# Branch blocks of a decoder layer: three joined products per block in banks of their own, summed over halves before the gates

## The reference, cut to what matters

```
merged = (jax.nn.sigmoid(ga) * (ya @ w_br_a[l])
          + jax.nn.sigmoid(gb) * (yb @ w_br_b[l])
          + jax.nn.sigmoid(gc) * (yc @ w_br_c[l]))
x = x + merged @ w_out[l]
```

## Time and profile before

| what | us |
|---|---|
| median of 3 runs | 2014.06 (2010.58 to 2015.64) |
| the profiled execution, its own time | 2014.7 |
| its span, first to last instruction | 2013.4 |
| TensorE busy in the span | 1774.1 (88%) |
| VectorE busy | 1555.3 (77%) |
| ScalarE busy | 932.5 (46%) |
| GpSimd busy | 650.5 (32%) |
| the branch blocks, start of the first and of the last matmul | 547.5 and 641.0 |

### The profile page before, as it was taken

One profiled execution on the slowest core, in us unless ns is written; L12 is line 12 of the kernel. 1 busy time (PEld: TensorE's weight loads), 2 busy tenths in 40 slices (PEclk: granted clock), 3 DMA queues, 4 the chain that ended last, 5 costly groups with the idle time before them and its releaser, 6 DMA issues.

```text
span 2013.4 us, 26324 instructions
## 1 busy us (share of the span) xinstructions
PE 1774.1 (88%) x9788; PEld 1532.3 (76%) x9788; DVE 1555.3 (77%) x2067; ACT 932.5 (46%) x1482; POOL 650.5 (32%) x558
## 2 busy tenths in 40 slices
PE   6999999999999999956776244499999999999998
PEld 5878888888899887756776244488888888888886
DVE  5575555555565548988988899988988989999997
ACT  5444444444543442123443899843444444343344
POOL 1000000001045003467777677122222224353452
PEclk9999999999999999978888555799999999999999
DMA  9556565656566869999999999588999999999995
GB/s 313 171 161 170 171 177 170 172 171 177 146 187 210 321 228 417 366 406 403 417 397 410 375 388 403 217 332 353 411 411 388 396 398 404 406 406 408 401 410 204
DMA packets 293970, 627.79 MB, mean 312 GB/s; under 512 B 10412, under 2 KB 223453, under 8 KB 235390
## 3 DMA queue, kind: packets, MB, share of 16 engines
q0 software_dynamic: 48400, 343.95, 42.3%
q1 hardware_dynamic: 244846, 281.15, 40.6%
q10 hardware_dynamic: 640, 1.63, 0.2%
HBM read 622.45 MB, written 8.44 MB: 313 GB/s over the span
## 4 chain that ended last, share of the span: by engine, by line
PE 68%; DVE 12%; ACT 5%; issue 5%; POOL 4%; DVEq 3%; DMA 3%; ACTq 0%; POOLq 0%
PE ps L2124 34%; PE ps L1767 12%; PE ps L1766 6%; DVE u_ring L1559 6%; PE ps L1966 4%; PE ps L1952 4%; DVEq L1509 3%; DMA u_ring<-in_peer_u,idx_all 2%; PE ps L1754 1%; PE ps L1763 1%; ACT ones L1157 1%; ACT w_hi L798 1%; POOL u_ring L718 1%; POOL u_ring L709 1%; PE ps L1891 1%
## 5 line engine op out<-in xcount | busy, mean ns | idle before, releaser
L1767 PE MATMUL ps<-act_both,w_hi 128*128 128x512 f32 x1200 | 427.1, 398 | 0.0
L1214 ACT ACTIVATE v_hi<-v_raw 128x2048 fp32r<-128x2048 f32 x128 | 245.6, 1919 | 388.8 <-PE ps L2124 198.2
L2124 PE MATMUL ps<-v_hi,c_hi 128*128 128x512 f32 x1008 | 392.2, 389 | 1.2 <-DVE c_lo L1638 1.2
L2124 PE MATMUL ps<-v_lo,c_hi 128*128 128x512 f32 x1008 | 392.1, 389 | 0.0
L2124 PE MATMUL ps<-v_hi,c_lo 128*128 128x512 f32 x1008 | 392.1, 389 | 0.0
L1300 DVE TENSOR_TENSOR w_lo<-raw,w_hi 128x2048 fp32r<-128x2048 f32 x111 | 257.2, 2317 | 159.9 <-ACT w_hi L798 159.8
L1559 DVE CUSTOM_DVE_ANT_0 u_ring<-u_ring,ps 128x2048 f32<-128x2048 f32 x144 | 326.2, 2277 | 21.9 <-DMA u_ring<-in_peer_u,idx_all 21.7
L798 ACT ACTIVATE w_hi<-raw 128x2048 fp32r<-128x2048 f32 x112 | 214.3, 1913 | 269.0 <-PE ps L1767 205.8
L1766 PE MATMUL ps<-act_both,w_lo 128*128 128x256 f32 x1200 | 338.4, 282 | 0.0
L1634 DVE TENSOR_TENSOR v_lo<-v_raw,v_hi 128x2048 fp32r<-128x2048 f32 x128 | 293.2, 2290 | 53.3 <-ACT v_hi L1214 52.7
L1767 PEld LDWEIGHTS ps<-act_both,w_hi 128*128 128x128 f32 x1200 | 226.7, 189 | 50.2
(11 more groups left out here) (265 smaller groups left out, 2693.6 us busy)
## 6 DMA issues: line engine op xcount, KB each, us to landing
v_raw<-in_peer_v SPq DMA_DIRECT2D x128, 1024.0 KB, 7.2
raw<-in_w_in SPq DMA_DIRECT2D x80, 1024.0 KB
raw<-in_w_out SPq DMA_DIRECT2D x16, 1024.0 KB
wq<-in_peer_w_q SPq DMA_DIRECT2D x8, 2048.0 KB, 11.3
raw<-in_w_br_a SPq DMA_DIRECT2D x16, 512.0 KB
bias_by_query<-bias_by_distance POOLq DMA_DIRECT2D x1, 4096.0 KB, 20.7
bias_st<-bias_by_query POOLq DMA_DIRECT2D x16, 256.0 KB, 4.7
raw<-in_w_br_b SPq DMA_DIRECT2D x16, 256.0 KB
```

The source lines that it names most:

```text
L1214: nc.scalar.activation(v_hi[hi_slot(b)][:, :], v_raw[b % RING][:, :], ACT.Copy).then_inc(vh_ok, 1)
L1767: last = nc.tensor.matmul(bank, *both, start=False, stop=(k == NK - 1))
L2124: last = nc.tensor.matmul(ps[:, 4 * t + c, :], c_parts[cp][j % v_slots[0]][:, t], v_parts[vp][j % v_slots[vp]][:, WIDE * c:WIDE * c + WIDE ...
```

## The change

- TensorE takes `by_pairs` for the branch blocks too: for each `k` one matmul of 512 columns and one of 256. Each branch has a bank of its own, banks 0 to 2 for even blocks and 3 to 5 for odd ones.
- VectorE reads the three banks with one `tensor_reduce`, which adds the halves and writes 768 elements a partition into `mtmp`. A new semaphore, `mj_ok`, tells TensorE after it that the banks are free (before: `m_mul`, after the products). A `drain` follows, and then one instruction multiplies gates and sums, both in SBUF, in place (`m_mul`).
- The low part of merged block `m` moves behind the low weights of the next block (`merged_low`); the last one stands behind the loop.
- GpSimd's and ScalarE's instructions and waits, SP's transfers, and TensorE's wait for all of `m_mul` behind block 15, are as before.

```diff
+        def merged_low(m, j):
+            dve.wait_ge(m_hi, m + 1)
+            nc.vector.scalar_tensor_tensor(out=mg_lo[:, span(T * m, T)], in0=msum[:, j], scalar=0.5,
+                                           in1=mg_hi[:, span(T * m, T)].bitcast(F32), op0=ALU.mult, op1=ALU.subtract).then_inc(m_lo, 1)
         def merge(i):
             for j in range(NRAW):
                 m = NRAW * i + j
                 dve.wait_ge(blk_done, m + (N_BR + 1))
                 wait(dve, m_sum, 2 * m - 2)
-                nc.vector.scalar_tensor_tensor(out=mtmp[:, j % 2, 0:2].rearrange("p g t -> p (g t)"), in0=gates[:, span(3 * T * m, 2 * T)],
-                                               scalar=1.0, in1=ps[:, J + j % 2, :], op0=ALU.add, op1=ALU.mult)
-                nc.vector.scalar_tensor_tensor(out=mtmp[:, j % 2, 2], in0=gates[:, span(3 * T * m + 2 * T, T)], scalar=1.0,
-                                               in1=ps[:, S_BANK + j % 2, 0:T], op0=ALU.add, op1=ALU.mult).then_inc(m_mul, 1)
+                nc.vector.tensor_reduce(mtmp[:, j % 2], ps[:, 3 * (j % 2):3 * (j % 2) + 3].rearrange("p g (h t) -> p g t h", h=2), AX.X,
+                                        ALU.add).then_inc(mj_ok, 1)
+                dve.drain()
+                products = mtmp[:, j % 2].rearrange("p g t -> p (g t)")
+                nc.vector.scalar_tensor_tensor(out=products, in0=gates[:, span(3 * T * m, 3 * T)], scalar=1.0, in1=products,
+                                               op0=ALU.add, op1=ALU.mult).then_inc(m_mul, 1)
                 low(NRAW * i + N_BR, j + 2)
-                dve.wait_ge(m_hi, m + 1)
-                nc.vector.scalar_tensor_tensor(out=mg_lo[:, span(T * m, T)], in0=msum[:, j], scalar=0.5,
-                                               in1=mg_hi[:, span(T * m, T)].bitcast(F32), op0=ALU.mult, op1=ALU.subtract).then_inc(m_lo, 1)
+                if not isinstance(m, int) or m > 0:
+                    merged_low(m - 1, (j - 1) % NRAW)
         peeled(dve, NK // NRAW, merge)
+        merged_low(NK - 1, NRAW - 1)
...
-                wait(pe, m_mul, NRAW * i + (j - 1))
+                wait(pe, mj_ok, NRAW * i + (j - 1))
...
-                by_column(ps[:, J + j % 2, 0:T], j % NHL, 0, 8, waits)
-                by_column(ps[:, J + j % 2, T:2 * T], j % NHL, 8, 12, waits)
-                by_column(ps[:, S_BANK + j % 2, 0:T], j % NHL, 12, NK, waits).then_inc(blk_done, 1)
+                by_pairs(ps[:, 3 * (j % 2)], j % NHL, 0, 8, waits)
+                by_pairs(ps[:, 3 * (j % 2) + 1], j % NHL, 8, 12, waits)
+                by_pairs(ps[:, 3 * (j % 2) + 2], j % NHL, 12, NK, waits).then_inc(blk_done, 1)
```

More of the change, by code:

```diff
@@ L411, in build @@
     y_lo = sem("y_lo")
+    mj_ok = sem("mj_ok")
     m_mul = sem("m_mul")
@@ L1746, in _, with wide_part @@
         w_wide = [w[:, :, :, :].rearrange("p s (a b) c -> p s a (b c)", b=WIDE // P) for w in w_parts]
[L1748 to L1758, removed]
+        def wide_part(bank, slot, k, k0=0, k1=NK):
             both, low_part = (w_hi[:, slot, k], act_both[:, k]), (w_lo[:, slot, k], act_hi[:, k])
-            if k == 0:
+            if k == k0:
                 nc.tensor.matmul(bank, *both, start=True, stop=False)
@@ L1766, in wide_part, with by_pairs @@
                 nc.tensor.matmul(bank[:, 0:T], *low_part, start=False, stop=False)
-                last = nc.tensor.matmul(bank, *both, start=False, stop=(k == NK - 1))
+                last = nc.tensor.matmul(bank, *both, start=False, stop=(k == k1 - 1))
             return last
-        def by_pairs(bank, slot):
-            for k in range(NK):
-                last = wide_part(bank, slot, k)
+        def by_pairs(bank, slot, k0=0, k1=NK, waits=None):
+            for k in range(k0, k1):
+                if waits is not None:
+                    waits(k)
+                last = wide_part(bank, slot, k, k0, k1)
             return last
```

## The result

| | before | after |
|---|---|---|
| median, us | 2013.39 (4 runs, 2010.58 to 2015.64) | 2027.11 (4 runs, 2026.52 to 2027.57) |
| the profiled execution's own time, us | 2014.7 | 2026.52 |
| its span, us | 2013.4 | 2025.2 |
| start of the projection, us | 642.57 | 649.44 |

The ratio is 1.0069, with a 95% interval of 1.0056 to 1.0082: the change makes the kernel some 14 us slower, where 6.8 were predicted. The time lies 0.1 us beyond the upper end of the range.

A forecast was written before the change was run, and what follows sets the result against it. TensorE was taken to bound the stage, busy 93.25 of 94.0 us. Blocks +3.1, end +2.2 and clock +1.5 made +6.8 on 2014.7: 2021.5, lowered 0.6 for the runs' median to 2020.9 us; range 2013 to 2027.

The forecast's parts named there:

- Matmuls, 5.60 us a block: TensorE's branch blocks: 5.60 us each with 512- and 256-column pairs, 0.16 less, 2.6 us over 16 blocks if TensorE keeps pace.
- Drain 0.07: VectorE, between reduction and products: the drain costs 0.07 us, an estimate between 0 and 0.1.
- Merged low part 0.35: VectorE, right behind low weights: 0.42 us less 0.07 overlap, assuming instructions issued back to back keep the port.
- Rival 2: GpSimd gets in between low weights and merged low part: 0.45 every second block, 2.7 us, giving 2023.6; chance 0.20.
- Two rings, 6.0 us a block: Branch blocks: from late high weights, ScalarE's ring of 5.86 and VectorE's of 6.03 exceed TensorE's 5.60; thirteen blocks add 3.2 us.
- The loop's starts, +0.9, less 0.5 for the first stalls: VectorE's 0.29 us at each of three loop starts joins its ring, +0.9; first stalls still growing take 0.5 off.
- The end, +2.2: TensorE's wait for block 15's products before the projection grows from 1.32 to 3.5 to 3.8 us: +2.2.
- The clock, +1.5 (0 to 3): Projection start: after 3.5 us idle TensorE runs at half clock for about 3 us, costing 1.5, bounds 0 and 3.
- The projection behind absorbs nothing: The projection behind the stage is paced by TensorE, so nothing in it absorbs the delay.
- TensorE keeps pace (0.22): Branch blocks: TensorE still sets the pace, as sums find gaps or VectorE's part is shorter; 2013.3 to 2014.8, chance 0.22.
- Weight loads (0.05): TensorE's blocks: weight loads are the limit, not columns; if a block falls to 5.2 us, 2007; chance 0.05.
- A clock that falls inside the stage (0.03): Half clock on a tenth of the stage's 94 us costs 5 us more: 2027; chance 0.03.

The follow-up runs named there:

- low_first: end_and_act with VectorE's next low weights between reduction and products, and a wait for `mj_ok` in place of the drain; 2015.94 us, ratio 1.0023.
- act_order: Kernel after, with ScalarE's high part of merged block m - 1 moved behind the high weights of block m + 2; 2019.79 us, ratio 1.0030.
- short_sums: Kernel after, with both GpSimd sums covering 16 of their 256 columns and `msum` cleared once ahead; 2016.13 us, ratio 1.0013.
- end_filler: Kernel after, with 14 unneeded matmuls between TensorE's last block and its wait for the products; 2020.77 us, ratio 1.0042.
- end_wait: Kernel after, with TensorE's wait before the projection on block 14's sum over halves instead of all products; 2023.07 us, ratio 1.0048.
- defer_only: Kernel before, with only the merged low part moved a block later; 2011.58 us against 2011.37 for before, ratio 1.0005.
- end_and_act: Kernel after with the edits of end_wait and act_order together; 2014.81 us, ratio 1.0027.
- end_wout: end_wait with the first `w_out` piece of the projection's second column group issued ahead of `x`, `g_ffn` and sub keys; 2017.18 us, ratio 1.0035.
- low_first_wout: low_first with the load order of end_wout; 2010.63 us against 2012.09 for before, ratio 0.9996.

## Why the prediction was wrong

**Step by step.**

- *Matmuls, 5.60 us a block:* right. *low_first* shows TensorE without idle and blocks 5.62 apart (592.42 less 586.80).
- *Reduction 1.76, products 0.96:* right (1745 and 959 ns).
- *Drain 0.07:* right in the pass with fixed numbers (1.83 us from the start of the reduction to that of the products, 565.60 to 567.43), too small by 0.1 in the loop. There, from the start of the reduction to that of the products it is 1.93 us, with 0.18 marked as issue. In *low_first*, which has no drain, the instruction behind the reduction starts after 1.84 (626.10 to 627.94). That is 0.1 us a block in VectorE's ring.
- *Merged low part 0.35 (0.42 less overlap):* this is **the step that failed**. It rested on the assumption that "instructions issued back to back keep the port". It is written in both rings and in VectorE's own 5.3. Measured: 0.95 in 15 of 16 blocks, because GpSimd's waiting sum gets the port between two VectorE instructions that follow each other at once. VectorE's ring without any wait is then 5.88 and not 5.3, shown by *act_order* (5.88 in every block), *short_sums* (0.44, stage 96.6) and *low_first* (0.42, stage 92.6). Rival 2 named this mechanism with a chance of 0.20, and priced it for every second block, at 0.45: 2.7 us in all. It is 0.53 in every block but the last, and that its 2.7 comes near the 2.9 that were missing is luck (next point).
- *Two rings, 6.0 us a block:* ScalarE's high weights do stand behind `mg_hi`, behind GpSimd's sum, but they hold VectorE up in every second block and not in each. The ring of 6.03 holds for those blocks: with 0.5 more for the merged low part and 0.1 for the drain it gives the 6.65 measured. In the others the high weights are there in time, the 0.67 for GpSimd's gap drops out, and VectorE's ring runs at 5.89. So the port and the drain cost some 0.6 us a block more than forecast, the alternation gave back 0.77 in every second one, and the mean of 6.27 is only 0.26 above the forecast 6.01 because two errors of opposite sign met. Over 13 blocks that is 3.4 us.
- *The loop's starts, +0.9, less 0.5 for the first stalls:* not borne out. At the three starts the reduction comes 0.87 us behind the start of the merged low part (602.15 to 603.02, for one), as in every other block: they cost nothing. The blocks cost +6.0 us (8.3 less 2.3) instead of +3.1; the 2.9 between them is, to 0.1, the 3.4 less the 0.4 of this term.
- *The end, +2.2:* right. The idle time is 3.64 instead of 1.32, +2.3.
- *The clock, +1.5 (0 to 3):* the mechanism was right, the term mis-sized: 2.4 us by *end_filler*. I had taken the 3 us of half clock at 547.5 for the length; here it was 5.6.
- *The projection behind absorbs nothing:* right for the delay itself. For a gain it is different: the projection of *end_wait* starts earlier and takes 5.4 us more than that of before (2.8 more than after, which itself has 2.4 of slow clock), and mostly the loads decide it.

The sum so corrected is 6.0 + 2.3 + 2.4 = 10.7, against 10.9 in the profiles and 11.3 to 16.5 by the ratio. What the lowest of these leaves over is below what the runs can tell.

**The shared port.** My error was about who comes next when GpSimd has been waiting and VectorE has its next instruction ready: I gave the port to VectorE, and the runs give it to GpSimd (0.95 us for a merged low part of 0.42). The Trainium skill (SBUF — State Buffer, section "Who interferes with whom") says that a VectorE instruction with two SBUF inputs contends with a GpSimd instruction that reads SBUF, that issue order decides who blocks, and that `tensor_reduce` never contends. The runs agree with the last: in *low_first* the reduction takes 1.76 us and the sum beside it 0.74, as they do alone.

**The other rivals.** TensorE keeps pace (0.22) didn't happen in the kernel after, but it is what *low_first* does, by the condition that I had put on it: the sums find a gap. Weight loads (0.05): no block came near 5.2 us; with all waits gone it was 5.6. A clock that falls inside the stage (0.03): it stayed at 1.00 there.

**What stays open.** The ratio of the kernel after allows 0.4 to 5.6 us more than the 10.9 that stage and projection show; no experiment looked at the gathers. Why the clock came back later in one kernel than in another after the same idle time, and what the 0.18 us behind the drain consist of, wasn't taken apart. The drain was never changed by itself: the 0.1 us is read from starts.

## What to carry to other kernels

When an instruction with two SBUF inputs joins others on VectorE while GpSimd has a sum in flight, write down for each GpSimd sum beside which VectorE instruction it will run. A sum of 0.74 us that had waited cost the next VectorE instruction 0.53, though the two VectorE instructions were issued back to back; only where VectorE had idle time behind it did that cost nothing (*defer_only*). Put the instruction that reads PSUM where the sums fall due. Of the 12.1 us between 104.7 and 92.6 that was worth 3.2 here (with the drain); 3.6 came from the end wait and 5.2 from ScalarE's order. And when a stage gets shorter, look at the queue of loads that waits for its last semaphore before counting the gain.

## What the runs showed that I had not expected

- A waiting GpSimd sum gets in at the first boundary between VectorE instructions, even when these are issued without a gap: 0.53 us on the merged low part, in 15 blocks of 16.
- The length of a wait doesn't fix what the clock costs. After 3.64 us of idle time the kernel after ran at 0.50 for 5.6 us and its projection took 94.2 us; *act_order*, after the same 3.64, had 0.69 in the row below (0.50 from 645.4 to 648.6 only) and 93.2 us; with the wait filled (*end_filler*, 0.43 idle) it was 91.7. Inside the projection the clock was 0.50 behind a stall of 2.26 us (*end_wait*), and stayed at 1.00 behind one of 1.47 (*end_and_act*).

```profile
644.49:650.00 5.51, 5.51 (x17) 4.37 (x18) 3.45 (x3) 0.42 (x1) 3.51 (x2) 0.69 0.77 280
```

- One transfer's place in SP's queue, moved past three others, was worth 4.2 us in *end_wout* and 6.0 in *low_first_wout*, and nothing in *before_wout*: it matters only once the projection starts earlier.
